# A fused Mamba-2, differential attention and mixer kernel: order of the first fetches, the first group's decays on ScalarE, and three moved or removed steps

## The reference

```python
h = rms_norm(x, norm_g);  zxbcdt = h @ w_in                     # dt_raw: its last 32 columns
xbc = silu(causal_depthwise_conv(xbc, conv_w, conv_b))
dt = softplus(dt_raw + dt_bias);  a = -exp(a_log)
# per chunk and head
acs = cumsum(a * dt);  seg = acs[:, None] - acs[None, :]
decay = exp(where(causal, seg, -inf))
y_diag = (C @ B.T * decay) @ (x * dt)
y_off  = (C @ state) * exp(acs)
state  = state * exp(acs[-1]) + B.T @ (x * dt * exp(acs[-1] - acs))
# second block
log_a = -8.0 * r * softplus(-lam);  a = exp(log_a)              # gates of the recurrence
u = silu(layernorm(u, ln_g, ln_b)) @ w_pw                       # long convolution branch
```

## Time and profile before

| | us |
|---|---|
| median of 3 runs | 1240.95 |
| lowest, highest | 1239.09, 1242.38 |
| profiled execution | 1243.29 |
| its span, first to last instruction | 1241.6 |
| TensorE busy in the span | 1224.8 |
| mean granted TensorE clock | 0.995 of full |

### The profile page before, as it was taken

The page is one execution under the profiler, slowest core; times in us unless marked ns, Lnnn a source line. Parts: engine busy times, 40 slices in busy tenths (PEclk is TensorE's granted clock), DMA queues, the critical chain, the costliest instruction groups (busy, mean ns, idle before and its releaser), DMA issues.

```text
span 1241.6 us, 17292 instructions
## 1 busy us (share of the span) xinstructions
PE 1224.8 (99%) x6181; PEld 994.1 (80%) x6181; DVE 869.9 (70%) x1342; ACT 593.5 (48%) x941; POOL 55.5 (4%) x48
## 2 busy tenths in 40 slices
PE   8989999999999999999999999999999999999997
PEld 6778888888888887878787899748888888888886
DVE  5888889888965366667767789997555422555776
ACT  6447656765663243655556563684332211223122
POOL 1101110111010000000000000000000000000000
PEclk9989999999999999999999999999999999999999
DMA  5433333333324322222222222114333233333322
GB/s 170 121 100 104 85 102 114 106 84 103 116 68 135 94 85 73 81 69 68 76 76 68 69 85 86 51 51 119 90 97 101 86 101 86 100 94 92 118 86 101
DMA packets 182605, 115.24 MB, mean 93 GB/s; under 512 B 3600, under 2 KB 175920, under 8 KB 181536
## 3 DMA queue, kind: packets, MB, share of 16 engines
q1 hardware_dynamic: 180672, 104.02, 28.9%
q0 software_dynamic: 1888, 10.62, 2.5%
HBM read 112.46 MB, written 2.16 MB: 92 GB/s over the span
## 4 chain that ended last, share of the span: by engine, by line
PE 91%; DVE 5%; ACT 1%; issue 1%; DMA 1%; SPq 0%; ACTq 0%; DVEq 0%
PE psum L546 65%; PE psum L1108 6%; PE psum L746 4%; PE psum L814 3%; PE psum L920 3%; DVE arena L2209 2%; PE psum L783 2%; PE psum L801 1%; PE psum L650 1%; PE psum L658 1%; PE psum L641 1%; DVE w_lo L1665 1%; PE psum L795 1%; DMA arena<-x 1%; PE psum L1059 1%
## 5 line engine op out<-in xcount | busy, mean ns | idle before, releaser
L1146 ACT ACTIVATE w_hi<-w_raw 128x1024 fp32r<-128x1024 f32 x184 | 194.4, 1057 | 420.6 <-PE psum L546 342.7
L1665 DVE TENSOR_TENSOR w_lo<-w_raw,w_hi 128x1024 fp32r<-128x1024 f32 x184 | 227.9, 1238 | 135.1 <-ACT w_hi L1146 134.7
L546 PE MATMUL psum<-a_hi,w_hi 128*128 128x512 f32 (+1 forms) x864 | 316.1, 381 | 0.6 <-DVE w_lo L1665 0.4
L546 PE MATMUL psum<-a_lo,w_hi 128*128 128x512 f32 (+1 forms) x864 | 311.6, 376 | 0.0
L546 PE MATMUL psum<-a_hi,w_lo 128*128 128x512 f32 (+1 forms) x864 | 310.1, 374 | 0.0
L546 PEld LDWEIGHTS psum<-a_hi,w_hi 128*128 128x128 f32 x864 | 157.8, 189 | 35.3 <-issue 4.7
L546 PEld LDWEIGHTS psum<-a_hi,w_lo 128*128 128x128 f32 x864 | 157.6, 189 | 30.4
L546 PEld LDWEIGHTS psum<-a_lo,w_hi 128*128 128x128 f32 x864 | 157.5, 188 | 28.9
L546 PE MATMUL psum<-b_hi,w_hi 128*128 128x512 f32 x376 | 150.6, 401 | 2.3 <-DVE arena L1999 2.3
L546 PE MATMUL psum<-b_lo,w_hi 128*128 128x512 f32 x376 | 149.3, 397 | 0.0
L546 PE MATMUL psum<-b_hi,w_lo 128*128 128x512 f32 x376 | 148.5, 395 | 0.0
(11 more groups left out here) (331 smaller groups left out, 1823.2 us busy)
## 6 DMA issues: line engine op xcount, KB each, us to landing
w_raw<-a_w_in SPq DMA_DIRECT2D x48, 512.0 KB, 3.8
w_raw<-w_up SPq DMA_DIRECT2D x32, 512.0 KB, 3.9
w_raw<-w_down SPq DMA_DIRECT2D x32, 512.0 KB, 3.8
arena<-acs POOLq DMA_DIRECT2D x8, 1024.0 KB, 5.0
w_raw<-a_w_out SPq DMA_DIRECT2D x16, 512.0 KB, 3.7
w_raw<-w_kv SPq DMA_DIRECT2D x16, 512.0 KB, 3.6
w_raw<-b_w_in SPq DMA_DIRECT2D x16, 512.0 KB, 3.9
w_raw<-w_in SPq DMA_DIRECT2D x14, 512.0 KB, 3.7
```

What stands on the lines that cost most here:

```text
L546: ins = mm(out, wv[:, u.par, k, :], xv[:, k0 + k, c0:c0 + cn], start=(first and begin and i == 0 and n == 0), stop=(last and end and i == ...
L1146: ac(w_hi[:, u.par, :, :], w_raw[:, u.par, :, :], ACT.Copy).then_inc(S["hi_ready"], 1)
L1665: tt(w_lo[:, u.par, :, :], w_raw[:, u.par, :, :], f32(w_hi[:, u.par, :, :]), ALU.subtract).then_inc(S["lo_ready"], 1)
```

## The change

SP: `w_dt` is fetched before quarter 3 of `x` instead of before quarter 2, and the wait for it is gone; VectorE, which uses it, waits for `raw0` at 32, which counts `w_dt` and the second weight unit together. TensorE: the first tile is cut after two k blocks instead of four. GpSimd: `exponents` of group 0 is gone. ScalarE: for group 0, `decays` makes the sixteen blocks itself, relu(-(acs_l) + acs_s) with the token's sum as bias, and the copy of the token sums comes after `hi` of the next unit. VectorE: in `group(Lin(1))` the weights, `weigh_x` and the states come sooner, `weigh_pairs` after the states, and `lo` of the fourth unit last; `gate_rates` moves behind the value evacuations and their `lo`. ScalarE's Silu of one column at L1548 is gone.

```diff
@@ -371,12 +371,11 @@
             for i in range(4):
                 if i == 1:
                     load(Lin(U_MAMBA), t["a_w_in"], 0, ssd_cols(Lin(0))[0])
-                if i == 2:
+                if i == 3:
                     sp.dma_start(wdt, t["w_dt"]).then_inc(S["raw0"], 16)
                 sp.dma_start(x_tok[:, :, 256 * i:256 * i + 256], t["x"].rearrange("(t p) d -> p t d", p=P)
                              [:, :, 256 * i:256 * i + 256]).then_inc(S[f"x_in{i}"], 16)
 
-            sp.wait_ge(S["raw0"], 16)
             group(Lin(0), 1)
             group(Lin(1))
             with sp.Fori(0, 3) as i:
@@ -484,7 +483,7 @@
                 pool.wait_ge(S["ab_in"], (s * 16 + 16).v)
                 nc.gpsimd.tensor_copy(gacs.rearrange("p (c h) -> p c h", h=HPG), tok[:, 0, :, ds((s * HPG).v, HPG)]
                                       ).then_inc(S["pool_own"], 1)
-                pool.wait_ge(S["pool_own"], (s + 1).v)
+                pool.wait_ge(S["pool_own"], s.v)
                 nc.gpsimd.tensor_tensor(mix, decay_in, gacs.rearrange("p (c h) -> p h c", h=HPG).unsqueeze(3)
                                         .to_broadcast([P, HPG, NT, P]), ALU.subtract).then_inc(S["seg_ready"], 1)
 
@@ -495,8 +494,6 @@
                                         ).then_inc(S["gadd_ready"], 1)
 
             spread(Lin(0))
-            pool.wait_ge(S["tok_ready"], 1)
-            exponents(Lin(0))
             with pool.Fori(1, GROUPS) as i:
                 pool.wait_ge(S["e_ready"], i * HPG)
                 pool.wait_ge(S["seg_ready"], i)
@@ -603,9 +600,9 @@
                 if k < 4:
                     warm(1)
             u, m = Lin(U_MAMBA), Lin(M_MAMBA)
-            tile_of(u, m, a_hi, a_lo, False, ks=range(4), ready=("x_lo", 1))
+            tile_of(u, m, a_hi, a_lo, False, ks=range(2), ready=("x_lo", 1))
             turn_x(range(6, KT))
-            tile_of(u, m, a_hi, a_lo, False, ks=range(4, KT), ready=("x_lo", 5))
+            tile_of(u, m, a_hi, a_lo, False, ks=range(2, KT), ready=("x_lo", 3))
             u, m = u + 1, m + 1
             tile_of(u, m, a_hi, a_lo, False, ks=range(3))
             pe.wait_ge(S["dtw_ready"], 1)
@@ -1213,12 +1210,23 @@
 
             def decays(s):
 
-                act.wait_ge(S["seg_ready"], (s + 1).v)
-
-                ac(mix, mix, ACT.Relu, scale=-1.0).then_inc(S["relu_done"], 1)
+                if s.reg is None and s.c == 0:
+                    act.wait_ge(S["ab_in"], 16)
+                    act.wait_ge(S["tok_ready"], 1)
+                    pairs = [(r, c) for c in range(NT) for r in range(HPG)]
+                    for r, c in pairs:
+                        ins = ac(mix[:, r, c, :], decay_in[:, r, c, :], ACT.Relu, scale=-1.0,
+                                 bias=tok[:, 0, c, r:r + 1])
+                        if (r, c) == pairs[-2]:
+                            ins.then_inc(S["relu_done"], 1)
+                    ins.then_inc(S["seg_ready"], 1)
+                else:
+                    act.wait_ge(S["seg_ready"], (s + 1).v)
+                    ac(mix, mix, ACT.Relu, scale=-1.0).then_inc(S["relu_done"], 1)
                 act.wait_ge(S["cb_ready"], (s + 1).v)
                 ac(b_tok.rearrange("p c n -> p (c n)"), bank(2)[:, 0:(NT - 1) * P],
                    ACT.Copy).then_inc(S["bt_ready"], 1)
+                act.wait_ge(S["seg_ready"], (s + 1).v)
                 act.wait_ge(S["relu_done"], (s + 1).v)
                 ac(mix, mix, ACT.Exp, scale=-1.0).then_inc(S["mexp_ready"], 1)
                 ac(stat[:, DEC:DEC + 8].rearrange("p (h c) -> p h c", h=HPG),
@@ -1245,9 +1253,11 @@
                     ac(row(b_hi, s * 2 + j, 0, SEQ), gun[:, j, :], ACT.Copy,
                        scale=ggate[:, 2 + j:3 + j]).then_inc(S["uh_ready"], 1)
 
-            def group(g):
+            def group(g, tokens=None):
                 u, s = g * 6 + U_MAMBA, g - 1
                 hi(u + 2)
+                if tokens:
+                    tokens()
                 first_tap(g, 0)
                 decays(s)
                 hi(u + 3)
@@ -1292,9 +1302,12 @@
             silu(g, 5)
             act.wait_ge(S["dt_acs"], 2)
             ac(dts[7][96:128, :], dts[7][96:128, :], ACT.Exp).then_inc(S["dt_exp"], 1)
-            act.wait_ge(S["dt_tp"], 1)
-            ac(tok[:, 0, :, :].rearrange("p b c -> p (b c)"), bank(6)[:, 0:P], ACT.Copy).then_inc(S["tok_ready"], 1)
-            group(Lin(1))
+
+            def token_sums():
+                act.wait_ge(S["dt_tp"], 1)
+                ac(tok[:, 0, :, :].rearrange("p b c -> p (b c)"), bank(6)[:, 0:P], ACT.Copy).then_inc(S["tok_ready"], 1)
+
+            group(Lin(1), token_sums)
             with act.Fori(0, 3) as i:
                 group(Lin(2, 2, i))
                 group(Lin(3, 2, i))
@@ -1545,7 +1558,6 @@
             gate_roots((2, 3))
             act.wait_ge(S["ln_stat"], 1)
             root(stat_at(N_SD), bnag[:, :, 1], eps2, 1.0, S["ln_sd"])
-            ac(stat[:, DEC + 2:DEC + 3], one, ACT.Silu)
             act.wait_ge(S["ln_shift"], 1)
             for i in range(NT):
                 ins = ac(lnt[:, i, :], bank(1 + 2 * (i // 2))[:, 256 * (i % 2):256 * (i % 2) + 256],
@@ -1715,7 +1727,7 @@
             lo(Lin(U_MAMBA))
             turned_low(range(2, KT))
             lo(Lin(U_MAMBA + 1))
-            dve.wait_ge(S["raw0"], 16)
+            dve.wait_ge(S["raw0"], 32)
             tt(wdt, wdt, par[:, C_ANORM:C_ANORM + KT].unsqueeze(2).to_broadcast([P, KT, 32]), ALU.mult
                ).then_inc(S["dtw_ready"], 1)
             turned_copies((2, 4, 6))
@@ -1888,15 +1900,22 @@
                     group_columns(s)
                 evacuate_in(g, 0)
                 lo(u + 2)
-                taps_of(g, 0)
                 if weights:
                     weights()
                     group_columns(s)
-                weigh_x(s)
-                evacuate_in(g, 1)
-                lo(u + 3)
-                weigh_pairs(s)
-                states(s)
+                    weigh_x(s)
+                    taps_of(g, 0)
+                    evacuate_in(g, 1)
+                    states(s)
+                    weigh_pairs(s)
+                    lo(u + 3)
+                else:
+                    taps_of(g, 0)
+                    weigh_x(s)
+                    evacuate_in(g, 1)
+                    lo(u + 3)
+                    weigh_pairs(s)
+                    states(s)
                 taps_of(g, 1)
                 evacuate_in(g, 2)
                 lo(u + 4)
@@ -2068,10 +2087,10 @@
                 else:
                     b_operand(range(4, KT))
                     lo(u + 3)
-                    gate_rates()
                     evacuate_values(n, 0)
                     evacuate_values(n, 1)
                     lo(u + 4)
+                    gate_rates()
                     evacuate(n, 3)
                     lo(u + 5)
                     return
```

## The result

The changed kernel takes 1231.2 us (median of 4 runs, 1230.8 to 1231.3), the kernel before 1241.7 (4 runs, 1239.1 to 1242.7). The ratio is 0.9918, 95% interval 0.9901 to 0.9936. The profiled execution took 1231.29 us, its span fell from 1241.6 to 1229.6, by 12.0.

What follows compares the result with a forecast made beforehand. TensorE, busy 1224.8 of 1241.6 us, was taken as the bound, so only its idle time or slow clock could be gained. Gains 6.7 + 4.0 + 0.75 + 0.9 = 12.35 off the median 1240.95 gave 1228.6 us, range 1226 to 1235.

Steps and rivals of the forecast that it cites:

- Part 1: First states, group 1: removing TensorE's wait before L641 gains 6.7 us, 3.4 idle and 3.3 clock; lower bound 3.0.
- The Relus: ScalarE's sixteen 128x128 ACTIVATEs with per-partition bias, first states: 0.29 us each, 4.8 us in all, 58.6 to 63.4.
- the pairs: VectorE's weigh_pairs after the first states: would end at 71.0, 0.8 us before TensorE needs it at 71.8.
- Part 2: First attention head: moving gate_rates ends TensorE's wait on L1999, gaining 2.3 us idle and 1.7 clock, 4.0 in all.
- Part 3: Layer norm: without the Silu at L1548, L1551 starts sooner and TensorE doesn't wait; gain 0.75 us, range -0.5 to +0.75.
- the row at 816.68: Profile row of a ScalarE table load that ran ahead of its Sqrt's wait; cited for the load before L1558's Silu.
- no slack is left: Layer norm: L1558's Silu would end just when TensorE's next four matmuls end; a waiting load restarts TensorE 0.5 us later.
- Part 4: The start: earlier fetches and the two-block cut remove TensorE idle stretches of 0.35 and 0.4 us; gain 0.9, bounds 0 and 0.9.
- rival C: Start: early fetch delays the last quarter of `x` up to 1.7 us, TensorE idles 1.5; time 1230.7, chance 0.06.
- rival A: First states: ACTIVATEs dearer or weigh_pairs late, TensorE still waits 1 to 2 us; gain 3.0, time 1232.3, chance 0.14.
- rival B: Layer norm: table load waits or a drain follows, giving -0.5 to -0.6 us; time 1229.9, chance 0.12.
- rival D: First states: ACTIVATEs at 0.94 us or more undo the gain; at 1.05 us about 1242.6, slower than before; chance 0.03.

Runs made afterwards that it cites:

- E5: Kernel before with only the sixteen Relus on ScalarE and the token sums' copy behind `hi`, VectorE's order left old: 1235.63 us, ratio 0.9951.
- E6: Kernel before with only VectorE's new order in `group`, GpSimd's subtraction left in: 1239.66 us, ratio 0.9982.
- E2: Kernel before with only `gate_rates` moved behind the value evacuations: 1239.12 us, ratio 0.9975.
- E3: Kernel before with only ScalarE's Silu of one column at L1548 taken out: 1241.09 us, ratio 0.9991.
- E9: Changed kernel with a one-column Copy on ScalarE between the wait for TensorE's L1028 and the Silu, so the table load must wait: 1232.19 us, ratio 0.9925.
- E4: Kernel before with only the fetch order, SP's wait gone and the first tile cut after two k blocks: 1240.00 us, ratio 0.9990.
- E7: Changed kernel with each of the sixteen Relus cut into two of 64 columns: 1234.17 us, ratio 0.9939.

## Why the prediction was right

The time lies in the range and the mechanisms were those forecast. Against the profiled execution the working had 12.35 us and the profile after has 12.0.

Part 1: 6.7 forecast. The states of the next group moved by 7.1 us, 0.75 of them from the start, so 6.4. The Relus, the covers and the pairs came within 0.3 us of the working. The prediction weighed ScalarE's half and VectorE's order as one step. E5 shows ScalarE's half to be all of it; the order alone (E6) gains 2.3.

Part 2: 4.0 forecast, 4.1 between the profiles before and after (from the first states of the next group, 112.77 and 105.63, the 30 matmuls begin 2.3 us sooner, and they take 1.83 less). E2's profiled span is 3.9 less than before's (another execution, at a clock of 0.996), and the second stall's idle and clock are gone from its trace.

Part 3: 0.75 forecast, and the wait of 0.75 is gone in E3. The load ran ahead of the wait, as the row at 816.68 had it, and E9 shows what it would have cost otherwise. The prediction's "no slack is left" was right too.

Part 4: 0.9 forecast, 0.75 in the profile after, 1.1 in E4, and 1.05 in both if the landing of `x` quarter 1 is taken out. The working took this landing as fixed; the turns that follow it started between 8.46 (E5) and 9.21 us (E3) in the thirteen profiles.

The step that was mis-sized is the last one of the sum: "1240.95 - 12.35 = 1228.6". It took the clock loss of the profiled execution (3.3 + 1.7 us) off the median. That execution is the slowest of the kernel before that was known then, at a clock of 0.995; in the group at 0.996, near the median, the loss is some 3 of those 5 us (1242.2 against the 1239.0 of the run at 0.999). The median of three that it was taken from, 1240.95, was also 0.6 us below the median of the 28 later runs. Idle time of 7.2 us and 3 us of clock make 10.2, measured 10.3 to 10.5. Taken off the profiled execution's own 1243.29, 12.35 gives 1230.9, against 1231.29 measured. The spread of the runs before, 3.3 us, was in sight, and was read as noise to be put on both sides of the range; it follows the clock, and is gone with the stalls (0.6 us among the changed kernel's runs). The time alone could not have told the mechanisms apart: 1231.2 is nearer to the 1230.7 of rival C, the 1232.3 of rival A and the 1229.9 of rival B than to the 1228.6 of the forecast. The traces rule these rivals out. One reading was off in rival D: 0.94 us from start to start is not the price of an ACTIVATE of four times the size (one of 128x512 takes 0.61 us) but of eight times (128x1024, 1.06 us).

## What to carry to other kernels

Where TensorE is the bound, a stall costs its idle time in every execution and a clock loss in some: take the first off any run (here it differed by up to 0.8 us where it hung on a DMA's landing), the second only off runs that had it, and compare the profiled execution's granted clock with that of the others before adding up. Where a VectorE instruction ends with a GpSimd instruction, look at whether both engines work on SBUF; here moving GpSimd's instruction to ScalarE, with one copy put behind the next `hi`, gave the whole gain, and reordering VectorE added nothing to it. In these traces a table load of ScalarE's ran ahead of a wait if no instruction that waits stood before it.

## What the runs showed of the hardware

The granted clock fell to the 1.2 GHz level behind idle times of TensorE of 2.3 and 3.4 us, and in E7 of 1.8 us. It did not fall behind the 1.3 us of E9, nor in E6's profile behind its 2.3 us (shown above) and over the whole stretch behind its 1.4 us:

```profile
57.00:85.00 28.00, 26.46 (x159) 21.83 (x159) 25.98 (x32) 15.25 (x19) 5.25 (x3) 1.00 0.40 120
```

Why the same stall loses more clock in one execution than in another is open; no run here separates it.
